# Two-block transformer on one core: the first tokens and the embeddings also arrive with features on partitions, the first weight tiles one by one, zeros through TensorE ahead of the work

## The reference

```python
h = rms_norm(x, attn_norm_g[l])            # x * rsqrt(mean(x*x)+eps) * g
proj = h @ w_in[l]                         # 1024 -> 416 | 512 | 256 | 512 | 3072 columns
c_q, c_kv, k_rope, gq, gk, gv, pool_in, gate_logits = split_columns(proj, IN_SIZES)
merged = gates0 * (o_mla @ w_branch_mla[l]) + gates1 * (o_gqa @ w_branch_gqa[l]) + gates2 * (o_pool @ w_branch_pool[l])
x = x + merged @ w_out[l]
x = x + (silu(u_gate) * u_val) @ ffn_w_down[l]   # u = conv(rms_norm(x) @ ffn_w_up[l])
```

## Time and profile before

| | |
|---|---|
| median of 3 runs | 1501.97 us (1501.68 to 1502.64) |
| the profiled execution's own time | 1503.06 us |
| its span | 1501.2 us |
| TensorE busy with matmuls | 1485.1 us (99%) |
| VectorE / ScalarE busy | 1048.5 us (70%) / 838.3 us (56%) |
| moved by the DMA queues | 255.83 MB, mean 170 GB/s |

### The profile page before, as it was taken

How to read it: one execution, slowest core, us unless ns; L and a number is a source line. 1 busy time by engine, 2 the same in 40 slices (tenths; PEclk the granted TensorE clock), 3 DMA queues, 4 the chain that set the end, 5 groups by cost and what they waited for, 6 DMA issues and landing times.

```text
span 1501.2 us, 22272 instructions
## 1 busy us (share of the span) xinstructions
PE 1485.1 (99%) x9024; PEld 1301.7 (87%) x9024; DVE 1048.5 (70%) x1565; ACT 838.3 (56%) x1244; POOL 60.6 (4%) x69
## 2 busy tenths in 40 slices
PE   8999999999999999999999999999999999999998
PEld 7877789998897778899989977998888888899886
DVE  6898778776578978787855567655467566766446
ACT  6465656655456565665644476554456555655435
POOL 1110000000021000000000001000000000100001
PEclk9999999999999999999999999999999999999999
DMA  7543445565555435455566533656656544555662
GB/s 250 191 143 124 142 155 190 189 195 187 192 163 169 138 111 174 158 190 185 182 197 206 169 99 113 218 183 193 190 163 226 171 121 136 175 169 187 206 186 80
DMA packets 73574, 255.83 MB, mean 170 GB/s; under 512 B 8448, under 2 KB 10112, under 8 KB 73472
## 3 DMA queue, kind: packets, MB, share of 16 engines
q1 hardware_dynamic: 73184, 254.25, 53.3%
q10 hardware_dynamic: 288, 0.17, 0.1%
HBM read 253.34 MB, written 1.05 MB: 169 GB/s over the span
## 4 chain that ended last, share of the span: by engine, by line
PE 93%; DVE 3%; ACT 2%; issue 1%; DMA 0%; POOL 0%; ACTq 0%; DVEq 0%
PE psum L1197 18%; PE psum L1201 18%; PE psum L1199 18%; PE psum L1190 10%; PE psum L1191 10%; PE psum L1188 10%; PE psum L1146 4%; PE psum L1347 2%; DVE w_low L2078 1%; PE psum L1377 1%; PE psum L1445 1%; ACT w_high L1600 1%; PE psum L1495 0%; DVE scratch L2060 0%; PE psum L1527 0%
## 5 line engine op out<-in xcount | busy, mean ns | idle before, releaser
L2078 DVE TENSOR_TENSOR w_low<-w_raw,w_high 128x1024 fp32r<-128x1024 f32 (+2 forms) x480 | 571.1, 1203 | 241.8 <-ACT w_high L1600 239.7
L1600 ACT ACTIVATE w_high<-w_raw 128x1024 fp32r<-128x1024 f32 (+2 forms) x480 | 496.4, 1043 | 313.9 <-PE psum L1201 213.7
L1188 PE MATMUL psum<-x_high,w_high 128*128 128x256 f32 x1056 | 299.5, 284 | 0.0
L1190 PE MATMUL psum<-x_low,w_high 128*128 128x256 f32 x1056 | 298.9, 283 | 0.0
L1191 PE MATMUL psum<-x_high,w_low 128*128 128x256 f32 x1056 | 298.9, 283 | 0.0
L1190 PEld LDWEIGHTS psum<-x_low,w_high 128*128 128x128 f32 x1056 | 202.7, 192 | 0.2
L1188 PEld LDWEIGHTS psum<-x_high,w_high 128*128 128x128 f32 x1056 | 202.7, 192 | 0.2
L1191 PEld LDWEIGHTS psum<-x_high,w_low 128*128 128x128 f32 x1056 | 202.7, 192 | 0.0
L1197 PE MATMUL psum<-w_high,x_high 128*128 128x512 f32 (+2 forms) x432 | 171.2, 396 | 1.4 <-DVE w_low L2078 0.9
L1199 PE MATMUL psum<-w_low,x_high 128*128 128x512 f32 (+2 forms) x432 | 164.9, 382 | 0.0
L1201 PE MATMUL psum<-w_high,x_low 128*128 128x512 f32 (+2 forms) x432 | 164.7, 381 | 0.0
(11 more groups left out here) (266 smaller groups left out, 2413.8 us busy)
## 6 DMA issues: line engine op xcount, KB each, us to landing
w_raw<-in_weights SPq DMA_DIRECT2D x450, 512.0 KB, 4.0
w_raw<-in_weights SPq DMA_DIRECT2D x16, 384.0 KB, 3.0
w_raw<-in_weights SPq DMA_DIRECT2D x8, 416.0 KB, 4.4
rows<-in_second_rows SPq DMA_DIRECT2D x4, 512.0 KB, 4.8
w_raw<-in_weights SPq DMA_DIRECT2D x6, 256.0 KB, 2.6
dil_masks<-in_consts SPq DMA_DIRECT2D x1, 768.0 KB, 6.1
residual<-in_x SPq DMA_DIRECT2D x2, 256.0 KB, 4.7
residual<-in_x SPq DMA_DIRECT2D x1, 512.0 KB, 6.7
```

The costliest lines, as they stand in the source:

```text
L1188: eng.matmul(o, wh[:, j, cut], high[:, k, :], start=k == 0 and f % 2 == 0, stop=False, skip_group_check=True)
L1190: eng.matmul(o, wh[:, j, cut], low[:, k, :], start=False, stop=False, skip_group_check=True)
L1600: act(self.unit_view(self.wh, u), raw, ACT.Copy).then_inc(sem("w_high"), 1)
L2078: tt(self.unit_view(self.wl, u), raw, self.unit_view(self.wh, u), ALU.subtract).then_inc(sem("w_low"), 1)
```

## The change

x is given a second time as `x_turned`, with features on partitions. Four transfers of 256 KB (two feature tiles each) bring it into the scratch memory; new steps `arrive` 0 to 7 make high (ScalarE) and low (VectorE) of one feature tile each from there. The 16 transposes of x are gone, and so is the first load of the identity. x with tokens on partitions is still loaded, in two halves of 512 KB, behind loads 4 and 5, and serves squares and residual.

The first four feature tiles of panel 0 are units of their own (416 floats per partition); units 2 and 3 share one load. Panel 0 has now units 0 to 5, panel 1 units 6 to 9, panel 2 units 10 and 11. `prefetch(n)` goes to n + min(5, n + 1). The squares stand behind unit 2, between splits 5, 6 and 7; `load_rows` of layer 0 behind unit 4; `constants` behind unit 6; `diag` behind unit 7, `row` and `tables` behind unit 8; `take_c`, `c_norm_a` and `c_norm_b` behind units 5, 6 and 7. All constants come in one transfer behind load 6, and the gains but the first 8 columns behind them.

VectorE writes zeros to a scratch tile first, and TensorE multiplies them three times (float32, 128 x 512) before it waits for anything else. The embeddings of both layers come with features on partitions; the transposes of `emb` are gone and each part is split by one instruction. Several semaphores are merged (`heads_summed`, `heads_rstd`, `rows_loaded`, `masks_loaded`, `small_loaded`), with counts that follow the list of steps.

```diff
@@ weight_units
-            for k0 in range(0, kts, step):
-                own.append(dict(name=name, layer=layer, source=source, panel=n, cols=cols, w=w, k0=k0,
-                                nk=min(step, kts - k0)))
+            first = [0, 1, 2, 3] if not units and not own else []
+            for k0 in first + list(range(len(first), kts, step)):
+                nk = 1 if k0 in first else min(step, kts - k0)
+                own.append(dict(name=name, layer=layer, source=source, panel=n, cols=cols, w=w, k0=k0, nk=nk))
...
-        u["n"], u["load"] = n, n
-        loads.append((at, size))
+        u["n"], u["from"] = n, 0
+        if n == 3:
+            u["from"] = loads[-1][1]
+            loads[-1] = loads[-1][0], 2 * size
+        else:
+            loads.append((at, size))
+        u["load"] = len(loads) - 1
@@ prefetch
-        while self.n_split <= min(n + min(SPLIT_AHEAD, n + 2), self.cap):
+        while self.n_split <= (last or min(n + min(SPLIT_AHEAD, n + 1), self.cap)):
@@ arrive
+        def later():
+            add("arrive", 4)
+            add("arrive", 5)
+            self.prefetch(0, 4)
+            add("arrive", 6)
+            add("arrive", 7)
+
+        for k in range(4):
+            add("arrive", k)
+            add("split", k)
+        self.n_split = 4
+        self.after(2, later)
+        self.after(3, lambda: (add("square", g, 0), add("mean", g), self.prefetch(0, 6), add("square", g, 1),
+                               add("rstd", g)))
+        self.after(7, lambda: add("constants"))
@@ mixing
-        add("load_rows", l)
-        self.after(4, lambda: add("diag", g))
-        self.after(6, lambda: add("row", g))
+        if l:
+            add("load_rows", l)
+        else:
+            self.after(5, lambda: add("load_rows", l))
+        self.after(8, lambda: add("diag", g))
+        self.after(9, lambda: add("row", g))
         add("pads", l)
-        self.after(4, lambda: add("tables", l))
+        self.after(9, lambda: add("tables", l))
@@ sync
+                if 1 <= n <= 3:
+                    load_arriving(n)
+                elif 4 <= n <= 5:
+                    c = slice((n - 4) * PANEL, (n - 3) * PANEL)
+                    eng.dma_start(self.x[:, :, c], src[:, :, c]).then_inc(sem(f"x_loaded{n - 4}"), 16)
+                elif n == 6:
+                    eng.dma_start(self.consts, dram["consts"][:, 0:N_HELD]).then_inc(sem("consts_loaded"), 16)
+                    eng.dma_start(self.cols[:, DK:N_FIRST_COLS], dram["first_cols"][0][:, DK:]
+                                  ).then_inc(sem("consts_loaded"), 16)
...
@@ tensor
-        q.wait_ge(sem("ident_loaded"), 16)
+        q.wait_ge(sem("dve_step"), 1)
+        for n in range(3):
+            eng.matmul(bank[7], self.junk[1][:, 0:P], self.junk[1], start=True, stop=True)
...
-                for i in range(2):
-                    for t in range(TT):
-                        d = turn(bank[6][:, i * SEQ + t * P:i * SEQ + (t + 1) * P], emb[:, t, i * P:(i + 1) * P])
-                d.then_inc(sem("emb_turned"), 1)
@@ scalar
+            elif kind == "arrive":
+                k, = key
+                q.wait_ge(sem(f"x_arrived{k // 2}"), 16)
+                act(self.features[STAGE_MIX[0]][0][:, k, :], self.arriving[:, k, :], ACT.Copy,
+                    scale=self.gain(STAGE_MIX[0])[:, k:k + 1]).then_inc(sem("arrived_high"), 1)
@@ vector
+        q.step(eng.memset(self.junk[1], 0.0))
...
+            elif kind == "arrive":
+                k, = key
+                high, low = self.features[STAGE_MIX[0]]
+                q.wait_ge(sem("arrived_high"), k + 1)
+                stt(low[:, k, :], self.arriving[:, k, :], self.gain(STAGE_MIX[0])[:, k:k + 1], high[:, k, :], ALU.mult,
+                    ALU.subtract).then_inc(sem("arrived_low"), 1)
```

More of the change, by code:

```diff
@@ L286, in __init__ @@
             self.pair_end[step] = n
+        sums = [step for step in self.steps if step[0] in ("c_norm_a", "g_scale_a", "mla_rstd_k", "mla_rstd_q")]
+        self.sums_end = {step: i + 1 for i, step in enumerate(sums)}
     def pairs(self, step):
@@ L855, in memory @@
         self.xn = self.y = by_token(self.scr[:, 0:TT * D])
+        self.arriving = by_tile(self.scr[:, 0:DK * SEQ])
         self.mix, self.ffn = [], []
@@ L1245, in tensor @@
                 b = TURN_BANKS[j]
[L1246 to L1250, removed]
+                self.x_ready(q, g, j // 2)
                 acquire(b)
@@ L1595, in scalar @@
                 size = u["w"] * u["nk"]
-                raw = self.raw[u["load"] % RAW_SLOTS][:, 0:size]
+                raw = self.raw[u["load"] % RAW_SLOTS][:, u["from"]:u["from"] + size]
                 q.wait_ge(sem(f"w_loaded{u['load'] % RAW_SLOTS}"), 16 * (u["load"] // RAW_SLOTS + 1))
@@ L1882, in scalar @@
                 l, = key
-                q.wait_ge(sem("emb_turned"), at(*step))
-                for i in range(2):
-                    d = act(self.ff[l][2][0][:, i, :], bank[6][:, i * SEQ:(i + 1) * SEQ], ACT.Copy)
-                d.then_inc(sem("emb_high"), 1)
+                q.wait_ge(sem("small_loaded"), 16 * (l + 2))
+                act(self.ff[l][2][0], self.ff[l][1], ACT.Copy).then_inc(sem("emb_high"), 1)
             elif kind == "take_up":
@@ L2100, in vector @@
                     q.wait_ge(sem("squared_odd"), at(*step) - 1)
+                else:
+                    q.wait_ge(sem("w_used"), 1)
                 c = slice(half * PANEL, (half + 1) * PANEL)
@@ L2245, in vector @@
                     sq.rearrange("p (t h d) -> p t h d", t=TT, h=MLA_H), AXIS_X, ALU.add
-                    ).then_inc(sem(f"m_{what}_summed"), 1)
+                    ).then_inc(sem("heads_summed"), 1)
             elif kind in ("mla_scale_k", "mla_scale_q"):
@@ L2494, in vector @@
                 q.wait_ge(sem("emb_high"), at(*step))
-                for i in range(2):
-                    d = stt(low[:, i, :], bank[6][:, i * SEQ:(i + 1) * SEQ], 1.0, high[:, i, :], ALU.mult, ALU.subtract)
-                d.then_inc(sem("emb_low"), 1)
+                tt(low, self.ff[l][1], high, ALU.subtract).then_inc(sem("emb_low"), 1)
             elif kind == "take_gate":
```

88 lines of the change are left out of this document (40 added, 48 removed).

## The result

The changed kernel takes 1504.59 us (median of 17 runs, 1503.69 to 1505.65); the kernel before, over 17 runs of its own, 1502.43 us (1501.48 to 1502.96). The ratio is 1.0017, 95% interval 1.001 to 1.0023: slower by 2.2 us, where 2.1 us less was forecast and the range ended at 1504.3. The profiled execution of the changed kernel is the fastest of its runs: 1503.69 us, span 1501.9.

What follows compares the result with a forecast made beforehand. TensorE, busy 99% of the span, was taken as the bound. 1.2 us gained at the start after row's stall plus 0.9 from embeddings made 2.1 us, 1501.97 to 1499.9 us; 8-in-10 range 1496.5 to 1504.3.

Steps and rivals of the forecast that it cites:

- The start: Kernel start to panel 0's end: no turned-token wait or x transposes; panel 0 ends at 16.0 against 21.86, 5.9 us sooner.
- The wait at row: TensorE at row, before panel 2: waits for VectorE's diag from 24.2 to 28.9, 4.7 us, leaving 1.2 us of gain.
- The time of load 9: L, load 9's landing, which starts the chain to diag: 21.0 at 390 KB/us; row starts at L + 7.9.
- the loads' own waits don't come later than the queue itself: Load 9's wait for the low of unit 6, at about 15.5, does not delay its landing beyond the queued bytes.
- The formula 22.2 - L: Gain at panel 2's start, from load 9's landing time L: 1.2 us forecast, -0.3 at 358 KB/us.
- The clock: Rival: TensorE's clock falls in the stall at row, about 2.6 us lost behind it; 1502.5 us, chance 0.28.
- Embeddings: Both layers' embeddings: four transposes gone from TensorE, 0.445 us in each layer, 0.9 us gained.
- The step from the profile to the median: Forecast median: 2.1 us taken off the runs' median 1501.97, 1.09 below the profiled run, giving 1499.9.
- Transfers set a slower pace: Rival: x twice slows the queue to 310 KB/us, load 9 lands at 25.3; 1504.2 us, chance 0.12.
- No wait at row: Rival: diag ready by 24.2, panel 2 at 27.4, sum 6.8 us, 1495.2; chance 0.15 including half a wait.
- The zeros don't lift the clock: Rival at the start: panel 0 takes up to 2.6 us more, swallowed by row's stall; same time as forecast.

Runs made afterwards that it cites:

- Both ways of taking it out: Changed kernel with layer 0's row behind unit 10 instead of 8, or its diag behind unit 4 instead of 7: 1498.71 and 1498.56 us.
- one moved step: Kernel before, whole, with layer 0's diag behind unit 5 instead of unit 3: 1510.80 us, against 1502.11 beside it.
- x loaded once: Changed kernel without the second transfer of x, ones in its place, so the output is not the reference's: 1504.66 us.
- the filled pause: Changed kernel with five float32 products, results overwritten, on TensorE ahead of its wait for diag: 1503.00 us.
- without the zeros: Changed kernel with the zeros neither written nor multiplied: 1504.13 us.
- x once and rows later: Changed kernel without the second transfer of x (ones instead) and with load_rows behind unit 7 instead of 4: 1501.89 us.
- the kernels with one moved step: Changed kernel with only row later (behind unit 10) or only diag earlier (behind unit 4): 1498.71 and 1498.56 us.

## Why the prediction was right and wrong

**The start** was right: first product at 6.40 (6 to 6.5 forecast), the zeros from 1.43 to 6.43 (1.3 to 6.1). Panel 0 ended at 17.07 instead of 16.0: TensorE waited 0.48 and 0.79 us for single tiles, where I had 0.7 in all, and load 2, with two tiles, held ScalarE up at 7.83. It cost nothing, since the pause at row swallowed it.

**The wait at row** was right in place, cause and size: 4.60 us forecast at 4.7, releaser diag. Both ways of taking it out give back about 6 us, and the kernel before gets it by one moved step. The chain from load 9's landing to row is 30.10 - 21.95 = 8.15 us (7.9 forecast).

**The time of load 9** was mis-sized by 1 us: 21.95 instead of 21.0. The step that failed is "the loads' own waits don't come later than the queue itself". I had the low of unit 6 at about 15.5; it was done at 17.02, since load 5, of the same unit, was issued at 7.27 and took 7.4 us to land. Load 9 was issued at 17.05, and 4.9 us to its landing followed, as with x loaded once. Over the whole stretch 6436 KB from 4.5 to 21.95 are 369 KB/us, but that average is no pace of the queue: it moved 337 to 361 GB/s from 5 to 10, 381 to 436 from 10 to 20, and 281 from 20 to 22. Load 11's chain was the later still, by 0.2 us, and I hadn't counted it. The formula 22.2 - L gives 0.25 us of gain instead of 1.2; the filled pause, in which the clock can't matter, measures 33.28 against 33.26, so 0.0.

**The clock** is the other step that failed: the sum put its fall at nothing, and I had it as a rival with 0.28, at 2.6 us. It fell in the profiled execution (0.71 granted from 28 to 32) and cost 1.4 us there, 4.73 us from row to panel 2 against 3.32 with the filled pause; by the medians the filled pause gives 1.6 back. None of the 17 runs shows more than 0.999 over the span, while nine of the eleven with the filled pause show 1.0. In the profiled execution the low level lasted 3 us; without the zeros, with x once and with x once and rows later it lasted 5 us and more, and row to panel 2 took 5.74, 5.98 and 6.07, so 2.4 to 2.8 us were lost. The rival's price was right, and the profiled execution, the fastest of its kernel, got off lightly. What the Trainium skill says in "TensorE: Matmul & The Clock Gate", Part 1, that idleness brings the clock back to half, is borne out (0.50 granted from 28 to 32 with x once and rows later). I had weighed the missing row of a fall as evidence against one, though the kernel before has no pause in which it could have shown.

**Embeddings**: 0.87 us of 0.9 forecast, by the part of the span behind panel 2.

**The step from the profile to the median** was wrong too. I took off the median what I had found against the profiled execution, 1.1 us above the median of three runs. But the start of the kernel before moves by more than 1 us between executions, while in the changed kernel row's wait makes the start anew: what the change removes from a slow start it doesn't remove from a median one. That reading is an argument from three traces (25.91, 26.68 and 27.33 at row); no run tests it by itself.

**The sum of the miss.** The profiled execution was forecast at 1500.96 and took 1503.69, 2.7 more: 1.4 for the clock, 1.2 for the gain at row that wasn't there, 0.1 left. The median was forecast at 1499.9 and is 1504.6, 4.7 more: these 2.7, the 1.1 by which I had set the median below the profile, and 0.9 by which the changed kernel's median lies above its profiled run. So the clock alone doesn't make the miss; with its rival's price the forecast would have been 1502.5. Where the 0.9 comes from is left open. The clock is likely a part of it: the seven runs of the changed kernel at 0.999 took 1503.69 to 1504.21, the ten at 0.997 and 0.998 took 1504.31 to 1505.65. But the filled kernel also spreads, from 1501.8 to 1503.9 with the clock up, so something ahead of row varies as well; no second trace of the same kernel shows it.

**The rivals.** "Transfers set a slower pace" was right in that row hangs on landings, and wrong in size: load 9 landed at 21.95, not at 25.3. "No wait at row" is what the kernels with one moved step have, at 1498.6 instead of 1495.2, for a new wait of 1.5 us for the key heads, panel 2 at 28.4 instead of 27.4, and the slow start of before that I had counted as a gain. "The zeros don't lift the clock": they do (a product every 0.19 us from 6.7 for every 0.35), for 0.2 us at most.

## What to carry to other kernels

When a list of steps is the order of all queues, a change of unit sizes renumbers every step that is placed by counting units: for each such step ask on every engine what now stands ahead of its producer, here c_norm_a and four more low parts ahead of diag. A fast start only moves the next meeting of two queues forward; look for the first place where the fastest engine waits for a step of a loaded one. Price a pause of TensorE with the slow clock behind it (here 1.4 to 2.8 us behind traced pauses of 3.2 to 5.9), ask of each load which instruction frees its buffer and not only how many bytes stand ahead of it, and judge a gain at the start of a kernel on medians, not on one traced execution.

## What the runs showed of the hardware

- After 4.6 us of idleness TensorE's products came every 0.43 us instead of 0.23 for 3 us in one kernel (0.71 granted over 28 to 32), and for 5.3 us in another after the same 4.6 us (x once). All five traces with a pause at row of 3.2 to 5.9 us show the fall. Five products whose results are thrown away, put into the pause, kept the clock at 1.00.
- The records don't show the slow stretch at a kernel's start: 1.00 is given for 10 to 11 us in the kernel before, where 416 columns take 0.34 us. The distance of two starts tells it.
- A float32 product of 128x512 takes two records of 0.83 us each at the low level (three products in 5.00 us) and half of it at the high one (five in 4.45).
- With x once, a load of 512 KB queued right behind a broadcast of 96 KB and 256 KB more took 8.0 us, against 4.8 and 5.4 for the two loads ahead of them, and from 21 to 23 the queue moved 142 GB/s. In the changed kernel a load issued 1.5 us behind the same transfers took 5.3 us.
- Panel 2 started at 31.91 us in one execution and at 33.26 in one of another kernel with the same steps up to there.
